# Sampled attention of a hybrid decoder step: small scores ahead of the prompt's last values, cached scores ahead of the first sampled values, second half's pages on SP's queue

## The reference

```
nsa_attend(q, gates, ...):                    # per sequence and key group (2 groups, 8 heads each)
    p_c = softmax(q . compressed keys)        # 31 compressed blocks
    p_s = softmax(q . selected keys)          # 512 cached keys (pages) + 4 new keys
    p_w = softmax(q . window keys)            # 512 cached keys (window) + 4 new keys
    out = g0 * p_c @ v_c + g1 * p_s @ v_s + g2 * p_w @ v_w
x -> out @ w_out -> layer norm -> ConvFFN -> ...
```

## Time and profile before

| what | us |
|---|---|
| median of 3 runs (lowest, highest) | 1748.54 (1742.39, 1749.49) |
| the profiled execution, its own time | 1739.84 |
| its span, first to last instruction | 1738.2 |
| PE busy in the span | 1616.9 (93%) |
| DVE, ACT, POOL busy | 997.8, 716.7, 304.1 |
| mean granted TensorE clock (1 is 2.4 GHz) | 0.964 |

### The profile page before, as it was taken

How to read it: one execution, slowest core, us unless ns; L and a number is a source line. 1 busy time by engine, 2 the same in 40 slices (tenths; PEclk the granted TensorE clock), 3 DMA queues, 4 the chain that set the end, 5 groups by cost and what they waited for, 6 DMA issues and landing times. The chain is left out here.

```text
span 1738.2 us, 31445 instructions
## 1 busy us (share of the span) xinstructions
PE 1616.9 (93%) x12602; PEld 1573.3 (91%) x12602; DVE 997.8 (57%) x1552; ACT 716.7 (41%) x1310; POOL 304.1 (17%) x758
## 2 busy tenths in 40 slices
PE   8999798978979999999998998799899999999985
PEld 8999677858979999999998998799899999999985
DVE  3345667754885445536557594758753464455662
ACT  4345666843444234323334337334342332243341
POOL 4610333530032012102200000002220120021000
PEclk9999899988999999999999999899899999999988
DMA  7644000052212222222221221231222222223211
GB/s 261 130 138 157 1 1 1 1 189 81 74 61 87 96 77 93 86 86 85 96 86 61 85 86 61 67 115 52 85 86 85 86 86 87 84 89 105 73 61 64
DMA packets 39946, 148.01 MB, mean 85 GB/s; under 512 B 6304, under 2 KB 6320, under 8 KB 39360
## 3 DMA queue, kind: packets, MB, share of 16 engines
q1 hardware_dynamic: 33264, 121.26, 21.6%
q0 software_dynamic: 6544, 24.81, 4.1%
HBM read 140.57 MB, written 9.10 MB: 86 GB/s over the span
## 5 line engine op out<-in xcount | busy, mean ns | idle before, releaser
L1821 PE MATMUL PS<-XH,HI 128*128 128x272 f32 (+1 forms) x1936 | 411.4, 294 | 42.7 <-DVE XL L1101 14.1
L1821 PE MATMUL PS<-XH,LO 128*128 128x272 f32 (+1 forms) x1936 | 405.0, 291 | 0.0
L1821 PE MATMUL PS<-XL,HI 128*128 128x272 f32 (+1 forms) x1936 | 404.0, 290 | 0.0
L1821 PEld LDWEIGHTS PS<-XH,HI 128*128 128x128 f32 x1936 | 310.6, 191 | 46.9 <-DVE LO L449 26.1
L443 ACT ACTIVATE HI<-RAW 128x1024 fp32r<-128x1024 f32 x223 | 235.4, 1057 | 279.0 <-PE PS L1821 256.0
L1821 PE MATMUL PS<-GH,HI 128*128 128x272 f32 (+1 forms) x1504 | 319.5, 294 | 25.3 <-DVE LO L449 9.6
L449 DVE TENSOR_TENSOR LO<-RAW,HI 128x1024 fp32r<-128x1024 f32 x223 | 272.1, 1221 | 100.8 <-ACT HI L443 100.5
L1821 PE MATMUL PS<-GH,LO 128*128 128x272 f32 (+1 forms) x1504 | 314.1, 291 | 0.0
L1821 PE MATMUL PS<-GL,HI 128*128 128x272 f32 (+1 forms) x1504 | 313.9, 290 | 0.0
L1821 PEld LDWEIGHTS PS<-XL,HI 128*128 128x128 f32 x1936 | 308.8, 191 | 0.1
L1821 PEld LDWEIGHTS PS<-XH,LO 128*128 128x128 f32 x1936 | 307.4, 190 | 0.0
(11 more groups left out here) (362 smaller groups left out, 1941.4 us busy)
## 6 DMA issues: line engine op xcount, KB each, us to landing
RAW<-in_w_stream SPq DMA_DIRECT2D x223, 512.0 KB, 3.3
ARENA<-in_cache_cmp POOLq DMA_DIRECT2D x32, 128.0 KB, 3.1
out_win_old<-in_win_copy POOLq DMA_DIRECT2D x1, 4064.0 KB, 18.5
X<-in_x SPq DMA_DIRECT2D x4, 544.0 KB, 7.0
X<-in_x POOLq DMA_DIRECT2D x1, 2176.0 KB, 9.1
out_y<-X POOLq DMA_DIRECT2D x1, 2176.0 KB, 6.9
ARENA<-in_cache_sel POOLq DMA_DIRECT2D x16, 128.0 KB, 2.8
ARENA<-in_cache_win POOLq DMA_DIRECT2D x4, 512.0 KB, 5.1
```

The costliest lines, as they stand in the source:

```text
L1821: ins = mm(PS[0:rows, b + h, 0:width], w[:, 0:rows], cols(x, x0 + n, h), start=first, stop=last)
```

## The change

Seven things are moved or added:

1. The four `other_scores` stand right behind `cached_scores(0)`, ahead of `values(15)`. They write banks 4 and 5 in place of 6 and 7, and count up a semaphore of their own, `small_done`; `s_done` is now counted up by `cached_scores`.
2. DVE copies the small scores of pieces 2 and 3 to SBUF (`LATER`, 2 x 96 columns at the unused end of XL) and reads them there.
3. `cached_scores(1)` stands behind `sample_trans(0)`, ahead of `sample_trans(1)` and of all sampled values.
4. `probs_t` and `cached_sums` of piece x lie in bank 6 + x % 2. The wait for the sum of the piece before moves from `sample_values` to `sample_trans` (piece x waits for the sum of x - 2); `sample_values(1)` stands ahead of `sample_trans(2)`.
5. DVE: `sample_max(2)` and `sample_max(3)` stand between the copies of pieces 0 and 1 and behind them, ahead of the sums and of the two splits. `out_lo(15)` stands behind the first two maxima. ACT: `out_hi(15)` stands behind `sample_exps(1)`, the splits behind `sample_exps(3)`.
6. `maxima(v)` has columns of its own for each piece.
7. The 16 pages of the second half are loaded by SP, each with its own read of the page number from SBUF, after `s_done` 56; SP then goes on as before. POOL's list has only the wait for `pv_done` 16 and the load of X left there.

```diff
@@ stream of SP
                 if c == C0["w_out"]:
+                    sp.wait_ge(page_landed, 16)
+                    sp.wait_ge(s_done, 56)
+                    for m in range(16):
+                        pg = sp.value_load(PAGE[0:1, 16 + m:17 + m], ...)
+                        sp.dma_start(kept(1, 0)[:, m // PAGES, m % PAGES, :], a["cache_sel"][bass.ds(pg * P, P), :])\
+                            .then_inc(cache_landed[1], 16)
                     sp.wait_ge(s_done, 64)
@@ POOL
-            pool.wait_ge(s_done, 64)
-            load_cache(1)
             pool.wait_ge(pv_done, 16)
@@ ACT
             sample_exps(0)
             sample_exps(1)
+            out_hi(15)
             sample_copy(0)
-            act.wait_ge(pv_done, 16)
-            splits.cap = C0["w_out"] + 2
-            splits.after(O0["w_out"] - 1)
             sample_copy(1)
             sample_exps(2)
             sample_exps(3)
+            splits.cap = C0["w_out"] + 2
+            splits.after(O0["w_out"] - 1)
             sample_copy(2)
             sample_copy(3)
@@ DVE
-            sample_max(0)
-            sample_max(1)
+            dve.wait_ge(small_done, 4)
+            for x in range(2):
+                chain.did(v.tensor_copy(LATER[x], small_scores(2 + x)))
+            for x in range(2):
+                chain.did(v.memset(PMS2[x], 0.0))
+                chain.sync()
+                sample_max(x)
+            out_lo(15)
             sample_copy(0)
+            sample_max(2)
+            sample_copy(1)
+            sample_max(3)
             sample_scales(0)
             sample_scales(1)
             sample_sum(0)
-            sample_copy(1)
+            sample_sum(1)
             splits.cap = C0["w_out"] + 2
             splits.after(O0["w_out"] - 1)
-            sample_max(2)
-            sample_max(3)
             sample_copy(2)
             sample_scales(2)
-            sample_sum(1)
             sample_copy(3)
```

More of the change, by code:

```diff
@@ L194, in kept @@
             return KEPT[hb][r].rearrange("p (b n c) -> p b n c", b=4, n=PAGES)
+        LATER = [nc.alloc_sbuf_tensor_at(f"LATER{e}", [P, 96], F32, offset=GH_AT - 4 * 256 + 384 * e)[:, :] for e in range(2)]
         PT2 = [t.rearrange("p (r k) -> p r k", r=2) for t in (XPR, KR)]
@@ L372, in small_scores, with probs_t @@
         def small_scores(v):
[L374 removed]
+            return PS[:, 4 + v % 2, 96 * (v // 2):96 * (v // 2) + 96]
         def fresh(pms, r, n=4):
             return pms[:, 160 * r:160 * r + n]
[L380 to L382 removed]
+        def probs_t(v):
+            return PS[0:96, 6 + v % 2, 0:384].rearrange("p (r q) -> p r q", r=3)
         def cached_sums(v):
[L386 removed]
+            return PS[:, 6 + v % 2, 0:192].rearrange("p (r d) -> p r d", r=3)
         def sample_out(hb):
@@ L846, in _ @@
             out_hi(14)
-            out_hi(15)
             def sample_exps(v):
@@ L1306, in _ @@
             out_lo(14)
[L1307 to L1310, removed]
             def sample_max(x):
@@ L1314, in sample_max @@
                 nm, nm2, _, _ = maxima(x)
-                pms, mb = PMS2[x % 2], small_scores(x)
-                dve.wait_ge(s_done, u + 1)
+                pms, mb = PMS2[x % 2], LATER[x - 2] if x >= 2 else small_scores(x)
+                dve.wait_ge(s_done, 65 + x // 2)
                 if x >= 2:
@@ L1337, in sample_copy @@
                     dve.wait_ge(pv_done, 16 + x - 1)
-                chain.did(v.tensor_copy(PTM2[x % 2][0:96], probs_t()))
+                chain.did(v.tensor_copy(PTM2[x % 2][0:96], probs_t(x)))
                 v.tensor_copy(PT2[x % 2][:, 0, :], PS[:, 4, :]).then_inc(pt_dve, 1)
@@ L1988, in cached_scores @@
                         for gg in range(2):
-                            mm(PS[32 * bb:32 * bb + 32, 2 * gg + r, :].rearrange("p (n c) -> p n c", n=PAGES),
-                               query(hb, gg, bb), kept(hb, r)[64 * gg:64 * gg + 64, bb, :, 0:P], start=True, stop=True)
+                            ins = mm(PS[32 * bb:32 * bb + 32, 2 * gg + r, :].rearrange("p (n c) -> p n c", n=PAGES),
+                                     query(hb, gg, bb), kept(hb, r)[64 * gg:64 * gg + 64, bb, :, 0:P], start=True, stop=True)
+                ins.then_inc(s_done, 1)
             def other_scores(x):
@@ L2004, in other_scores @@
                                  KS[rows, at:at + 4], start=True, stop=True)
-                ins.then_inc(s_done, 1)
+                ins.then_inc(small_done, 1)
             def sample_trans(x):
@@ L2068, in _ @@
             cached_scores(0)
+            pe.wait_ge(pt_act, transposed(64))
+            pe.wait_ge(pt_dve, transposed(64))
+            other_scores(0)
+            other_scores(1)
+            other_scores(2)
+            other_scores(3)
             for quarter in range(4):
                 values(15, quarter)
+            pe.wait_ge(negmax_ready, 66)
             pe.wait_ge(ot_lo, 15)
-            other_scores(0)
+            sample_trans(0)
+            cached_scores(1)
             pe.wait_ge(ot_lo, 16)
-            other_scores(1)
-            sample_trans(0)
+            sample_trans(1)
             sample_values(0)
[L2078 to L2083, removed]
+            sample_values(1)
             sample_trans(2)
-            sample_values(1)
             sample_trans(3)
```

9 lines of the change are left out of this document (6 added, 3 removed).

## The result

The changed kernel took 1734.38 us in the median of 8 runs (1729.01 to 1742.1), the kernel before 1746.15 us in 8 runs beside them: ratio 0.9936, with a 95% interval of 0.9917 to 0.9954. The profiled execution took 1731.86 us with a span of 1730.3. A later comparison on another chip (first experiment) gave 0.9961 (0.9941 to 0.9981). The change is a gain of some 0.4 to 0.6%.

A forecast was written before the change was run, and what follows sets the result against it. A dependent chain through DVE, ACT and PE was taken to set the time ahead of w_out, whose start moves from 406.4 to 398.0. These 8.4 us off 1748.54 give 1740.1 us; range for 8 in 10, 1733 to 1748.

The forecast's parts named there:

- rival A: In the new chain's holes PE keeps 2.4 GHz: 10.4 us gained, 1738.1 us; chance 0.17.
- The schedule: New chain laid out step by step from the cached scores: w_out starts at 395.9 at full clock, 398.0 taken.
- the 1.2 us for four small scores: PE's four other_scores ahead of values(15), at some 0.3 us each, 1.2 us in all.
- The clock: PE from 372.5 on partly at half clock: w_out at 398.0, against 395.9 at full and 399.5 at half.
- The small scores' copies: DVE's two copies of 128 x 96 from PSUM: 0.45 us for both, bounds 0.1 and 2 x 0.55.
- values(15): On PE behind the small scores, ends at about 369.9 instead of 368.8, before the maximum that the transpositions wait for.
- Item 3 and its wait: cached_scores(1) starts at 373.5, right when exponentials 1 end, released by ACT and not by a DMA.
- four holes: PE's idle stretches in the new chain, 1.3, 0.9, 2.3 and 3.6 us.
- SP's pages: SP's 16 page loads from 337.04 at 1.16 us each, out by 355.6, nothing late.
- rivals B and C: SP's pages late: 2.1 us each gives 1743.9 us; 3 us each gives 1758.3; chance 0.07 each.
- Rival D: DVE's list order makes PE's steps wait: w_out near 402, 4 us gained, 1744.5 us; chance 0.14.
- any place outside 337 to 410 changes: Sign that the forecast is wrong: a length changes outside 337 to 410 us of the span.

The follow-up runs named there:

- e1: The first experiment: the changed kernel run once more with no edit, on another chip; ratio to the kernel before 0.9961.
- e6: Changed kernel with SP's loads of weight chunks 23 and 24 held until the small scores are done; ratio to the kernel before 0.9941.
- e3: Changed kernel with item 7 undone, the second half's pages back on POOL after s_done 64; ratio to the kernel before 0.9997.
- e2: Kernel before with item 7 alone, the pages loaded by SP; ratio to the kernel before 1.0021.
- e4: Changed kernel with item 3 undone, cached_scores(1) behind sample_values(0) and ahead of sample_values(1); ratio to the kernel before 1.0009.
- e7: Changed kernel with DVE's two splits moved behind sample_copy(2) and sample_scales(2); ratio to the kernel before 0.9959.
- e10: Changed kernel with chunk loads held, only chunk 23's split kept early, sample_copy(0) ahead of out_lo(15), sample_values(1) waiting for negmax_ready 66; ratio to the kernel before 0.9951.
- e12: Kernel of e10 with sample_values(1) waiting for negmax_ready 68 again; ratio to the kernel before 0.9939.
- e11: Changed kernel with sample_values(1) waiting for negmax_ready 66 in place of 68; ratio to the kernel before 0.9946.
- e8: Changed kernel with DVE's third split moved behind sample_out_lo(1); ratio to the kernel before 0.9960.
- e5: Changed kernel with the small scores moved behind values(15), still into banks 4 and 5; ratio to the kernel before 0.9983.
- e9: Changed kernel with DVE's two splits behind sample_scales(2) and the third split on ACT and DVE behind the last sampled output; ratio to the kernel before 0.9939.

## Why the prediction was right

The forecast was 1740.1 us from a before of 1748.54, which is 8.4 less. By the ratios, times 1746, it gained 11.2 us (8.0 to 14.5) and, in e1, 6.8 (3.3 to 10.3). The stage gave 7.2 and 8.65. I predicted w_out on before's scale, at 398.0; the stage of 36.68 put on before's start gives 399.2, e1's 397.7. The measured time, 1734.38, is 5.7 us under the forecast and 1.4 above the lower end of the range (1733): 2.4 of the 5.7 are the kernel before, whose median is 1746.15 in the eight runs and was 1748.54 in three, the rest is gain beyond 8.4. The runs alone could not tell the forecast (8.4) from rival A (10.4); the stage's rows do. Of the first 11.2 us, 2.5 to 4 have no cause in the stage; the spread ahead of it is large enough for them, but that they come from there is not shown.

**The schedule came, 2 us late.** Times from the stage's start, predicted and measured in the changed kernel's profile: small scores at DVE 3.1 and 4.9; first maximum 6.1 and 7.9; exponentials 1 end at 11.0 and 12.8; third maximum 15.4 and 17.4; fourth 18.5 and 20.4; the two LO splits end at 24.3 and 26.1; sample_trans(3) 25.5 and 27.6; w_out 33.4 (at full clock; 35.5 taken) and 36.7. Of the 2.1 us by which sample_trans(3) is late, 1.8 are there at the first step. This is the term that I left out: the 1.2 us for four small scores were the matmuls alone, and PE stopped for 1.77 us in them (e6 ties the stop to the loads beside it). The rest, 3.3 - 2.1 = 1.2, came behind sample_trans(3), which ran at half clock.

**The clock** I had at 2.1 of a possible 3.6 us; it took 1.2, and the stop that I had not thought of, with what is late behind it, 2.1. The forecast of 35.5 for the stage is near 36.7 and 35.2 partly by luck: the clock cost less than allowed, and the stop took what it left and more. The order of the steps, their releasers and the three long holes behind the first were right; the sum came out because two wrong sizes pull against each other. Rival A (clock holds, 10.4 us) was half right: the rows at 370 to 384 have full clock, but part of values(15) and sample_trans(3) do not; e6, free of the stop and with full clock in sample_trans(3), comes to 9.85.

**The small scores' copies** took 0.42 us for both (364.89, the memset behind them at 365.37); 0.45 was taken. **values(15)** ended at 10.6 instead of 7.4: it ran partly at half clock, and first maximum and exponentials, late themselves, hid all but 0.4 us.

**Item 3 and its wait.** cached_scores(1) started when ACT released it, as predicted. Its times put four holes ahead of sample_trans(0), cached_scores(1), sample_values(1) and sample_trans(3), of 1.3, 0.9, 2.3 and 3.6 us. The last three were measured at 1.00, 2.25 and 3.75, each ended by the engine named. The first is missing in the first profile, where values(15) filled it, and 1.35 in e1. The 0.58 ahead of sample_trans(1) lies in the predicted times too (375.5 to 376.0), but was not counted among the holes. Item 3 needs item 7 (e3, 42.3), item 7 alone brings nothing (e2, 43.2), and without item 3 nothing of the gain is left (e4, 44.0).

**SP's pages** cost 1.13 us from issue to issue (335.62 to 352.57 in 15 steps), 1.16 was taken; rivals B and C needed over 1.86. The last issue was over at 352.9, before the window. Of the 1.13 us the issue itself takes 0.33, so 0.80 us are left between issues (0.62 on POOL). The Trainium skill (DMA: Bandwidth & Descriptors, Latency and other measured facts) gives a register load from memory some 600 ns; the trace agrees roughly. X's load came 7.6 us earlier (371.08 against 378.68), not 9: it waited for PE.

**Rival D** (DVE's order takes 4 us back) did not come: no step behind the first lost more than 0.3 us to DVE's list beyond the forecast. The splits do stand in the way (3.75 us), but e7 shows that they can't simply go, since the third chunk's load hangs on them.

**Elsewhere** the program did not change in length by more than the runs vary. But "any place outside 337 to 410 changes" was a poor test: the changed kernel's own two profiles differ by 8.8 us in the stretch ahead of the stage, and all 14 by up to 11.3.

## What to carry to other kernels

When a chain through four engines sets the time, lay it out step by step with measured durations and compare times from the stage's own start; a span of one profile says less than the edit is worth. Moves that hand a resource to each other can be worth nothing alone (early pages without early scores; two splits moved while the third chunk waits for them), so test them in pairs before dropping one. A wait that looks idle may be hiding the next one: taking away 2.25 us here made the wait one step on 2.45 us instead of 0.49.

## What the hardware showed

- PE stopped for 1.37 to 2.07 us inside a burst of short matmuls, ahead of its last four, in eight profiles of eight in which loads of chunks ran beside it, and at the same place for 0.18 to 0.27 in the three in which they were held (e6, e10, e12). In all eleven PE goes on 1.29 to 1.50 us after the end of one 16 KB packet of the instruction queue. The Trainium skill (Runtime: NRT & Kernel Launch, Instruction fetch mechanics) describes instructions as fetched in blocks through a DMA queue of each engine, and says that the fetch is hidden. The packets here fit the blocks; if it is the fetch that PE waited for, it was not hidden. e12 had another such stop of 2.05 us ahead of sample_trans(2). A packet of that queue ended 1.6 us before PE went on there too, but the DMA engines were idle around it: why it came so late, full DMA engines don't explain.
- The stretch ahead of the change took 360.0 to 371.3 us in kernels that are the same there. The seven late profiles (368.5 to 371.3: e1, e2, e4 to e7, e11) had a clock of 0.83 or 0.84 in 260 to 300; the seven early ones, before among them (360.0 to 365.3), had 0.87 to 0.96.
- The hole ahead of sample_trans(3) was followed by half clock wherever it was 3.06 to 3.75 us (changed, e3, e4, e8, e11). Behind 2.40 (e6) the clock was full, behind 2.54 and 2.69 (e1, e5) it was partly half. One of 1.50 was followed by full clock in e7 and e9 and by half clock in e10 and e12. In e6, e7 and e9, with full clock there, sample_trans(2) ahead of the hole had run wholly or partly at half clock (1.94, 1.84 and 1.64 us for eight). No rule that I could form from these rows tells the two apart.
